# Projections of a hybrid decoder step: four staging places per group, the samples' projection three chunks later, and a new order of taps, pooling and small pieces

## The reference, cut to what matters

```
h = rms_norm(x) ; z = h @ w_in                      # 1024 columns in
c_q, c_kv, k_r, u_pool, u_conv, gate = split(z)     # 256 | 128 | 32 | 256 | 512 | 1024
q = rms_norm(c_q) @ w_uq                            # 8 heads of 64 + 32 (the 32 rotated)
k, v from rms_norm(c_kv) with w_uk, w_uv            # latent attention, causal
pooling: trailing means (2, 4, 8, 16) of u_pool, minus the token, times pool_w
conv: a = u1 * sigmoid(u2); causal depthwise conv of width 31 (the "taps"),
      LayerNorm, silu, pointwise matmul
out = x + rms_norm((concat(attention, pooling, conv) * silu(gate)) @ w_out)
```

## Time and profile before

| what | us |
|---|---|
| median of three runs | 1366.24 |
| the profiled execution, its own time | 1370.15 |
| its span | 1368.3 |
| PE busy in the span | 1271.4 (93%) |
| DVE busy | 827.6 (60%) |
| ACT busy | 619.2 (45%) |
| POOL busy | 473.3 (35%) |

### The profile page before, as it was taken

The page is one execution under the profiler, slowest core; times in us unless marked ns, Lnnn a source line. Parts: engine busy times, 40 slices in busy tenths (PEclk is TensorE's granted clock), DMA queues, the critical chain, the costliest instruction groups (busy, mean ns, idle before and its releaser), DMA issues. The chain is left out here.

```text
span 1368.3 us, 21115 instructions
## 1 busy us (share of the span) xinstructions
PE 1271.4 (93%) x7426; PEld 1052.5 (77%) x7426; DVE 827.6 (60%) x1735; ACT 619.2 (45%) x1259; POOL 473.3 (35%) x408
## 2 busy tenths in 40 slices
PE   7879899989957999999999999988879999999998
PEld 6656777868745888888888888865668888888885
DVE  3477876876755988888888888834232424242412
ACT  6423343342225777777777777734321212121211
POOL 6335337263530532514324240059221313131302
PEclk9988999999977999999999999989889999999999
DMA  8427025250331233224232232572452322222211
GB/s 272 132 31 242 33 89 181 74 196 16 106 131 57 53 92 92 62 63 103 51 90 56 72 70 50 166 225 74 136 185 87 98 88 95 90 94 91 95 48 40
DMA packets 140479, 137.77 MB, mean 101 GB/s; under 512 B 55381, under 2 KB 110646, under 8 KB 138902
## 3 DMA queue, kind: packets, MB, share of 16 engines
q1 hardware_dynamic: 133238, 112.19, 27.7%
q0 software_dynamic: 4784, 15.71, 4.1%
q10 hardware_dynamic: 2352, 8.52, 2.0%
HBM read 100.15 MB, written 46.71 MB: 107 GB/s over the span
## 5 line engine op out<-in xcount | busy, mean ns | idle before, releaser
L1756 ACT ACTIVATE pT<-tp 128x512 fp32r<-128x512 f32 (+2 forms) x320 | 168.6, 532 | 106.4 <-PE tp L1695 97.0
L1813 DVE TENSOR_SCALAR_CACHE_REDUCE prob<-sc 128x512 f32<-128x512 f32 (+2 forms) x320 | 193.1, 604 | 31.8 <-PE sc L1687 17.6
L1822 DVE TENSOR_TENSOR big<-tp,pT 128x512 fp32r<-128x512 f32 (+2 forms) x320 | 193.9, 607 | 27.5 <-ACT pT L1756 27.0
L2471 PE MATMUL m<-w_gate,q2a 128*128 128x512 f32 x768 | 180.5, 394 | 3.6 <-POOLq L2449 3.6
L1695 PE MATMUL tp<-ident,prob 128*128 128x128 f32 x1088 | 171.7, 273 | 1.1 <-DVE big L1822 1.1
L1746 ACT ACTIVATE prob<-prob,nm 128x1024 f32<-128x1024 f32 (+2 forms) x192 | 171.7, 894 | 1.3 <-DVE nm L1816 0.7
L2471 PEld LDWEIGHTS m<-w_gate,q2a 128*128 128x128 f32 x768 | 144.5, 190 | 33.3 <-POOLq L2449 3.7
L1000 DVE SCALAR_TENSOR_TENSOR acc<-aT,cols,acc 128x512 f32<-128x512 f32 x232 | 163.3, 751 | 9.3 <-DVE qst L1080 1.3
L2633 DVE SCALAR_TENSOR_TENSOR shared<-m,rq,g_post 128x512 f32<-128x512 f32 x32 | 22.6, 747 | 233.8 <-POOL rq L2443 233.8
L1695 PEld LDWEIGHTS tp<-ident,prob 128*128 128x128 f32 x1088 | 128.6, 141 | 25.1 <-issue 1.7
L1212 PE MATMUL mm<-big,w_in 128*128 128x512 f32 x576 | 141.0, 403 | 4.5 <-ACTq L714 4.2
(11 more groups left out here) (324 smaller groups left out, 2274.5 us busy)
## 6 DMA issues: line engine op xcount, KB each, us to landing
xraw<-in_xT SPq DMA_DIRECT2D x17, 512.0 KB, 4.4
LAT<-in_cache_ckv SPq DMA_DIRECT2D x128, 64.0 KB, 2.1
k2a<-Y SPq DMA_DIRECT2D x16, 512.0 KB, 5.5
shared<-in_x SPq DMA_DIRECT2D x16, 512.0 KB, 4.4
out_y<-shared SPq DMA_DIRECT2D x16, 512.0 KB, 2.9
xtok<-in_x ACTq DMA_DIRECT2D x14, 512.0 KB, 4.7
raw<-QT SPq DMA_DIRECT2D x7, 1024.0 KB, 5.2
QT<-qst SPq DMA_DIRECT2D x24, 256.0 KB, 4.1
```

The source lines that it names most:

```text
L1756: act.activation(pT[0][:, 4 * c:4 * c + w // P, (t % 4) * P:(t % 4 + 1) * P], tp[n % NTP][:, 0:w].rearrange("p (k q) -> p k q", q=P), ACT. ...
L1813: dve.tensor_scalar(prob[:, slot[m % J], 0:w], sc[b][:, 0:w], -1.0, None, ALU.mult, ALU.min, accum_out=top).then_inc(sc_free[b], 1)
L1822: dve.tensor_tensor(cut(1), tp[n % NTP][:, 0:w].rearrange("p (k q) -> p k q", q=P), f32(cut(0)), ALU.subtract)\
L2471: last = pe.matmul(out, w(pw_, k), x(px, k), start=(k == 0 and q == 0), stop=(k == n - 1 and q == 2))
```

## The change

The places: five instead of four are known. Groups 0 to 2 go round four of them (two halves of `qst`, two halves of `yn`); the last group goes round five, with `aS` as the fifth. Since `normalise` writes into `yn`, it now waits, in every group, until the stores from both halves have landed (`in_yn`).

The samples' rows of the first product: PE ran them after each of the eight chunks of `x`; now they follow three chunks behind and end with three steps after the last chunk. Their split on ACT and POOL moves from chunk 0 to chunk 1.

ACT copies the four token rows of group 0 earlier, ahead of their squares. DVE's `samples_conv` is cut into its two halves, which move from ahead of `latents_lo` into the loop over the heads, in front of heads 1 and 4. Other taps of group 0 move with them. The gate of the next group, `gate_in(A, 0)`, comes before the remaining taps and the kept history. Thirty taps instead of 28 run before the latents' normalisation in groups 1 and 2, and 34 in the last. On POOL the last group's pooling comes before the ten copies, and `inv_std` before the copies of the last group.

```
-        q_place = (qst[:, 0, :], qst[:, 1, :], yn_flat[:, GROUP:], aS...[:, 0:GROUP])
+        q_place = (qst[:, 0, :], qst[:, 1, :], yn_flat[:, GROUP:], yn_flat[:, 0:GROUP], aS...[:, 0:GROUP])
-            order += [(("Q", g, h), (0, 1, 3 if g else 2)[h % 3]) for h in range(HEADS)]
-            order += [(("V", g, j), (0, 1, 3 if g else 2)[(HEADS + j) % 3]) for j in range(TILES)]
+            at = (0, 1, 2, 3, 4, 0, 1, 2, 4, 0, 1, 4) if g == GROUPS - 1 else (0, 1, 2, 3) * 3
+            order += list(zip([("Q", g, h) for h in range(HEADS)] + [("V", g, j) for j in range(TILES)], at))
+        in_yn = lambda g: [(b, QP.upto(b, [(kind, g, n) for kind in "QV" for n in range(HEADS)])) for b in (2, 3)]
...
 normalise (DVE)
-                    elif A.g == 0:
-                        dve.wait_ge(q_out[2], 16 * QP.used[2])
+                    for b, count in in_yn(max(A.g, 0)):
+                        dve.wait_ge(q_out[b], 16 * count)
...
 DVE, group 0
                 pool_in(A, 1)
-                samples_conv()
                 latents_lo(A)
...
                 for h in range(HEADS):
-                    run(A, 1)
+                    if h in (1, 4):
+                        samples_conv(h // 4)
+                    else:
+                        run(A, 2 if h else 1)
                     head_out(A, h)
...
                 run(A, 8)
                 stats(S)
-                run(A, CONV_OPS, CONV_OPS - 6)
+                run(A, 4)
                 normalise(S)
+                run(A, 3)
 
                 for g in range(1, GROUPS):
                     A, B = G[g], G[g - 1]
+                    A.wait(dve, "rb", 1)
+                    gate_in(A, 0)
                     run(B, CONV_OPS)
                     keep_history(B)
-                    A.wait(dve, "rb", 1)
                     A.earlier(dve, "a_free")
-                    gate_in(A, 0)
...
-                    run(A, 28)
+                    run(A, 34 if A.last else 30)
...
 POOL, end of the stage
+                pooling(A)
                 A.wait(pool, "hT_free", 1)
                 first_head(range(GROUPS - 1))
                 first_values(0, GROUPS - 1)
-                pooling(A)
+                inv_std(A)
                 first_head([GROUPS - 1])
                 first_values(GROUPS - 1, GROUPS)
-                inv_std(A)
...
 PE, first product
+                LAG = 3
                 for k in range(KC):
                     pe.wait_ge(w_lo, W_TOK + k + 1)
+                    A.wait(pe, "split", k + 1)
+                    for j in range(3):
+                        last = token_step(A, mm[MM.at[("z", 0, j)][0]], j, k)
+                    if k == LAG:
+                        S.wait(pe, "split", 1)
+                    if k >= LAG:
+                        last = token_step(S, mm[MM.at[key][0]], 0, k - LAG)
+                for k in range(KC - LAG, KC):
+                    last = token_step(S, mm[MM.at[key][0]], 0, k)
```

More of the change, by code:

```diff
@@ L174, in stage1 @@
         tb_done, tb_free = ([sem(f"tb_{n}{i}") for i in range(2)] for n in ("done", "free"))
-        q_in, q_out = ([sem(f"q_{n}{i}") for i in range(4)] for n in ("in", "out"))
+        q_in, q_out = ([sem(f"q_{n}{i}") for i in range(5)] for n in ("in", "out"))
         k_in, k_out = ([sem(f"k_{n}{i}") for i in range(2)] for n in ("in", "out"))
@@ L442, in _ @@
                 sp.wait_ge(s["s_out"], 16 * (1 + CC))
-                for b in range(4):
+                for b in range(5):
                     sp.wait_ge(q_out[b], 16 * QP.used[b])
@@ L1328, in _ @@
                 A = G[0]
-                banks = [(A, j, ("z", 0, j)) for j in range(3)] + [(S, 0, ("z", -1, 0))]
-                for _, _, key in banks:
-                    into(key)
+                LAG = 3
+                key = ("z", -1, 0)
                 for k in range(KC):
                     pe.wait_ge(w_lo, W_TOK + k + 1)
-                    for B, j, key in banks:
-                        if B.smp or j == 0:
-                            B.wait(pe, "split", 1 if B.smp else k + 1)
-                        last = token_step(B, mm[MM.at[key][0]], j, k)
+                    A.wait(pe, "split", k + 1)
+                    for j in range(3):
+                        last = token_step(A, mm[MM.at[("z", 0, j)][0]], j, k)
                         if k == KC - 1:
-                            full(last, key)
+                            full(last, ("z", 0, j))
+                    if k == LAG:
[4 more added lines that the diff above has]
+                    last = token_step(S, mm[MM.at[key][0]], 0, k)
+                full(last, key)
                 rows_of(A, 3)
```

36 lines of the change are left out of this document (17 added, 19 removed).

## The result

The changed kernel takes 1353.03 us (median of four runs, 1351.61 to 1354.90), the kernel before 1366.15 us on the same chip: a ratio of 0.9897, interval 0.9878 to 0.9917. In a later session, beside the experiments, it took 1354.32 us: 0.9903, interval 0.9876 to 0.9929. So it is about 1% faster, some 6 us short of the forecast and inside the range. The profiled execution took 1352.98 us. Between the two profiled executions 17.2 us were won, between the medians 13.1: the profiled execution of before lay 3.9 us above its median, so the differences between the rows are too large by about as much, all together.

A forecast was written before the change was run, and what follows sets the result against it. PE was taken to set stage 1's pace (busy 358.6 of 417 us), with 31.4 us of large idle times. Terms -3.5, -3.5, -4.5, -2 and -5.6 sum to -19.1 us: 1347 us, range 1337 to 1360.

The forecast's parts named there:

- the heads of group 0: From the samples' queries to block 0 of group 1: convolution among the heads and four places, -3.5 us, bounds -1 and -5.5.
- The start: Kernel start to the samples' queries: ACT's new order and samples three chunks behind, -3.5 us, bounds -1 and -4.5.
- The wait for the latents: PE's 7.13 us wait for DVE's bank ahead of group 0's heads: PE goes on 5.6 us earlier, wait under 2.
- they take the place of waits in this loop, so the loop stays as long as it was: DVE's loop over group 0's heads: 7.9 us of added convolution and taps replace 7.6 us of waits.
- Group 1: Group 1's early stretch: earlier gate and samples' normalisation remove 2.54 and 0.97 us waits and 1.3 us slow matmuls; -4.5 us, bounds -2, -5.5.
- one of two things that would make it wrong: Sign against the forecast: DVE standing for long before `normalise` because of the stores from `yn`.
- The heads of groups 1 and 2: Heads of these two groups: four places remove about half the waits for stores, -2 us, bounds 0 and -5.
- The last group: Last group's heads to its end: POOL's new order and more early taps, -5.6 us, bounds -3 and -7.5.
- the pooling's wait: PE's 2.37 us wait in the last group: pooling ends 5.9 us earlier without the ten copies, so it goes.
- The wait for `y`: PE's 4.08 us wait in the last group: six more early taps end before the last head, so it goes.
- Transfers bind: Rival: head stretches bound by transfers, not places; only -9 us, 1357 us; chance 0.17.
- A clock that stays up everywhere: Rival: PE's clock stays up nearly everywhere, all terms at their far bounds, 1338 us; chance 0.12.

## Why the prediction was right, and where not

In the two profiles the terms of the table sum to -16.7 and -14.6 us, where -19.1 was forecast; the heads of group 0 make nearly all of that difference.

- **The start** was right: -3.7 and -3.8 us where -3.5 was forecast. The channel blocks started at 37.46 instead of 36.8, since the lost waits cost 1.6 us and not 0.9. So 2.1 us came from the earlier start and 1.6 from the clock: the 60 matmuls took 14.10 us at a granted clock of 1.00, before 15.67 at 0.89. The forecast's own parts, 2.7 and 1.4, sum to 4.1; its term was lower.
- **The heads of group 0** are the term that was mis-sized: -1.2 and +1.3 us for -3.5, at and beyond the end of its bounds. In four more executions with the same code up to there it came to -1.4, +0.1, -2.6 and -4.1 against the one trace of before. The wait for the latents went as forecast (7.13 to 1.42). The step that failed is "they take the place of waits in this loop, so the loop stays as long as it was". From first to last head output DVE's loop took 20.6 us, before 17.6. Some 7.3 us of work came in, about as counted, but only 4.3 us of waits went: 1.5 of the 7.6 counted lay ahead of head 0, and 1.84 for a store remained. The experiments show the step. Three of them have the convolution ahead of the heads and all else as changed: there it took 34.1 to 35.4 us from the samples' queries to block 0, with the state stores early or late; in all others 37.0 to 42.3. DVE's waits for stores among the heads go with the places (4.80 us with three, none to 2.65 in the six executions with four) and with the state stores, in whose 15 us the heads now fall (no such wait in the two runs with these late). But with the convolution there, neither three places nor late state stores moved block 0 beyond the scatter. The forecast saw that POOL's loads would not move with the heads: the first left at 94.44 instead of 98.31, earlier by the gain of the start alone. It took the 9.9 us load of the earlier trace rows as given. That load, too, shared its time with the two state stores, which took 11.1 and 14.8 us in the trace of before. What slowed it was not asked, though the run that put these stores elsewhere won 7 to 8 us in the median.
- **Group 1** was right in the two profiles: -4.7 and -4.1 for -4.5, and 30.89 us with the gate put back. The wait of DVE for the stores from `yn`, forecast as 0 to 4 us with cover until PE wants `y`, was 6.28 and 7.33 and used up that cover (0.46 and 1.17 us of PE). The forecast had named it as one of two things that would make it wrong, and in other executions of the same code it did come: with 7.92 and 6.91 us of it PE lost 2.73 and 3.41, and the term came to -1.0 and -0.4, beyond its bound of -2. With 5.87 it was -5.1. So the size was right in part by luck: the wait was missed by about 2 us or more. What the forecast left out there is POOL's loads for group 2, which leave at the same time as those stores (4.3 to 5.2 us to landing, 2.3 to 2.4 in the runs where these loads leave later).
- **The heads of groups 1 and 2** came to -1.4 and -2.2 us for -2. The cause is open: with three places again, group 2 had its 3.05 us wait and lost 1.0 and 0.5 us by it, and nothing else moved.
- **The last group** was right in size (-5.7 and -5.8 for -5.6), by other parts. `normalise` does follow the statistics (1.43 us of waiting instead of 6.67), and the pooling's wait is gone: from the end of the transposes to tokens to the transposes back it took 5.2 us less, for 5.3. But PE's transposes to tokens did not end 1.3 us earlier against the heads; they ended 1.0 later (26.9 us behind the start of the heads instead of 25.9). The wait for `y` did not go (2.75 us), and the first key store landed at 381.48 and not early: the forecast had PE's transposes end only 1.3 us earlier because ACT's second half would have to wait, and took off 1 us for the copies. The trace has that bank's wait at 7.69 us; moving the store showed that SP's order made more than half of it. What made up for this stands in no part of the forecast: from the transposes back to the end of the pointwise product it took 8.0 us instead of 9.5, at a granted clock of 1.00 instead of 0.74: the 8 transposes took 1.07 us instead of 1.94 and the 6 matmuls behind them 1.65 instead of 2.91. That the sum was met is luck.
- **The rivals.** "Transfers bind" (1357) was the nearest in time. It is what happened in part to group 0, and to the first key store of the last group. A clock that stays up everywhere did not come: 0.95 in this window.

What stays open: why stage 2, whose code is the same, takes 944 to 948 us from one execution to the next, why POOL's old order costs 5.9 us in the trace and nothing in the median, and what three places are worth with the convolution ahead of the heads.

## What to carry to other kernels

Before a stretch is pulled forward, ask which transfers it will then share its time with: here ten microseconds won ahead of the heads put them beside stores in pieces of 60 and 120 bytes, which nothing waits for until the last group and beside which the transfers of every queue took longer. Move such stores behind the loads and issue a store when its data is ready, not in the order of a list; two small moves of that kind won some 8.7 us where the whole change had won some 13. And price a step on the engine that takes over the work, not only on the one that is relieved.

## What the hardware showed beside that

- Stores in small pieces slowed the transfers beside them, whoever issued these: 240 and 120 KB took 10.2 and 15.0 us, and between 85 and 95 us the engines were 0.78 busy at 41 GB/s, with the stores elsewhere 0.36 at 82 GB/s. Loads and stores of 256 and 512 KB from three queues took 7.7 to 12.8 us instead of 4.6 to 4.8.
- The same DVE product of two SBUF tiles took 1.19 to 1.20 us where POOL's splits waited for late loads, and 2.60 to 2.78 beside these splits once the loads were early.
- Of the 16.65 us by which stage 1 is shorter, 8.1 are the same 1557 matmuls in less time, with a mean clock of 0.95 instead of 0.93 of 2.4 GHz; 8.5 are time in which PE stood still.
